# State space layer of a two-layer decoder step: sample states in one run over four row groups, and the silu of B's convolution moved into the next turn

## The chip, the cores and the metric

The kernel runs on one core of a Trainium2 chip. The metric is the device time of one execution in microseconds; lower is better. The median of three runs is 2458.46 us (2457.54 to 2460.95).

## The reference, cut to what matters

One inference step of a two-layer decoder for a prompt of 512 tokens and a sample group of 8 sequences with 8 new tokens each, 576 tokens side by side. Four half SwiGLU networks, a state space (Mamba-2) layer and an attention layer follow one another. The change is in the state space layer alone. Per group of 4 heads, with the prompt cut in chunks of 128 tokens and each sample sequence a chunk of its own:

```python
xc = silu(conv_b + sum(xpad[:, k:k + l] * conv_w[k] for k in range(CONV_W)))   # split into x, B and C
a_cum = cumsum(dt * a)                       # inside the chunk
decay = exp(a_cum[q] - a_cum[s]) where s <= q
wts = (C @ B.T) * decay * dt                 # [q, s] per head
y = wts @ x + (C @ h_prev) * exp(a_cum) + d_skip * x
xw = exp(a_cum[-1] - a_cum) * dt * x
states = B.T @ xw                            # 128 x 64 per head and chunk
h = exp(a_cum[-1]) * h_prev + states         # ssm_prompt, ssm_sample
g = y * silu(z); g = g * rsqrt(mean(g * g)) * norm_g
x += g @ w_out
```

## The kernel before

Every large product is made of float32 operands split in a high and a low part (fp32r): weights arrive raw (`raw`, two slots), ScalarE casts the high part (`high_part`, L939, tile `wh`), GpSimd subtracts it for the low part (`low_part`, L782, tile `wl`), and TensorE multiplies high by high (L1523), high by low (L1524) and low by high (L1531). A unit is a 128 x 1024 block of weights; a slot of `raw` is loaded again by SP's queue when GpSimd is done with it.

The layer runs over 8 groups g. Group 0 is written out, groups 1 to 6 are one hardware loop (called turns 1 to 6 here), group 7 is written out. Each engine has its own program, ordered by hand, and they meet by counting semaphores. In turn g the projections of group g+1 are made ahead (`ahead(0)` to `ahead(5)`: two tiles of x, B, C, and two gate tiles) and the out-projection of group g-1 (`back(0)`, `back(1)`) is made behind.

TensorE's order in a turn: `decays(g)` (L1764, four banks 4 to 7, waits for the square root and for the fourth add of the sample states of the turn before), `back(0)`, `sample_decays` (L1768), `ahead(0)`, `turn` (L1778 transposes x, x and B tile by tile, each waiting for the silu of its tile, `xc_ready`; L1782 transposes the sample tokens), `ahead(1)`, `chunk_sums` (C times B, L1790, and for the samples L1792; chunk states L1798), `back(1)`, `ahead(2)`, `outputs` (L1810, L1820, L1823, for the samples L1828), `ahead(3)`, `states(g, 0)` (L1885), `ahead(4)` with `group_sums` (L1893) in its middle, `states(g, 1)` (L1885), `ahead(5)`.

The sample states: the 64 sample tokens of a group lie on 64 partitions, and `bd` holds B once for each of 4 sequences, masked to the tokens of sequence n and n + 4. A product of 32 partitions with `xws` gives one sequence's state. Two row groups of 32 partitions hold sequences 0 to 3 and 4 to 7. `states(g, half)` makes four sequences, in banks 6 and 7; VectorE adds them to `h0` by two adds (`sample_states`, L2873) before the other half may use the banks.

VectorE's order at the end of a turn: the outputs (`ysb`), `ahead(3)` (projection output to `xp`, L2685 to L2687), the sum of the squares (L2879, input of L1893), `sample_states(0)`, reciprocal (L2902), gain (L2905), `sample_states(1)`, `ahead(4)` (L2707), the low part of the gated output (L2913), `conv(g+1, 2)` (three taps, L2698), `ahead(5)` (L2707), then in the next turn `back(0)` to `back(3)` (L2727).

ScalarE: casts `high_part` (L939); at a turn's end the square root (L1343), silu of the two x tiles, casts of the gated output (L1355), gate silu, silu of B's convolution (`conv_out(g+1, 2)`), gate silu; at a turn's start the cast for `ahead(0)`, `exp_cum` for four heads (L1282, L1284), a cast, exponentials (L1304, L1291, L1308), the cast for `back(1)`, silu of C's convolution (`conv_out(g, 3)`, L1254, L1257, L1258).

SP's queue issues in order: `store_samples` (L639) waits for the four adds of a group, and behind it stand the weights' loads of the next turn's `ahead(0)` and `ahead(1)` (L565).

Before the loop VectorE computes dt and its sums, `state_coefs` (L2665 to L2670) and `head_rows` (L2714, tile `acm`), and GpSimd clears the padding (L822, L823), copies the convolution state (L831) and then makes the low parts.

## Time and profile before

| | |
|---|---|
| median of three runs | 2458.46 us |
| profiled execution, first to last instruction | 2457.2 us |
| TensorE matmul busy | 2421.8 us (99%) |
| VectorE busy | 1856.6 us (76%) |
| ScalarE busy | 1391.8 us (57%) |
| GpSimd busy | 731.7 us (30%) |
| the state space layer | about 392 to 943 us of the span |
| mean granted TensorE clock | 0.994 |

Busy time counts instructions, not waits. TensorE's products overlap in the records: the next one starts before the one before has ended. A row of the timeline gives the start from the span's beginning, the time from the first start to the last end of the merged instructions, engine, line, operation, output and inputs by the program's names, tile shape (rows*columns of the array), operand shape, count, and in brackets the idle time before it and what ended it.

### The profile page before, as it was taken

What the parts mean: (1) busy time and instruction counts of PE and PEld (TensorE: products, weight loads), DVE (VectorE), ACT (ScalarE), POOL (GpSimd) and SP (SyncE); (2) the same over time, 40 slices, a digit from 0 to 9 for tenths busy, and PEclk for the clock granted to TensorE, in tenths of its full rate; (3) what the DMA queues carried; (4) which work ended last, traced back from release to release, by engine and by line L of the source; (5) the groups of instructions that cost most, each with busy time, mean ns of one, the idle gap of its engine ahead of it and who ended that gap; (6) DMA issues with size and microseconds to landing.
All of it is one profiled execution on the core that took longest, in us unless ns stands there. A gap on an engine that the chain in (4) does not pass through costs nothing.

```text
span 2457.2 us, 50185 instructions
## 1 busy us (share of the span) xinstructions
PE 2421.8 (99%) x19713; PEld 2363.8 (96%) x19713; DVE 1856.6 (76%) x3053; ACT 1391.8 (57%) x2388; POOL 731.7 (30%) x672
## 2 busy tenths in 40 slices
PE   8999999999999999999999999999999999999998
PEld 8999999889999989999999999999999997999998
DVE  8979767988888888978876988875235438988875
ACT  7757553645555556757665767664222227767663
POOL 1222233444454532222223222224322321222222
PEclk9999999999999998999999999999999999999999
DMA  6677743123333325677665676763443334677762
GB/s 191 163 169 172 167 119 114 47 95 106 105 101 102 97 88 132 167 160 172 159 146 128 161 168 165 173 150 124 157 141 124 136 110 105 161 170 163 173 149 89
DMA packets 105558, 339.00 MB, mean 138 GB/s; under 512 B 13648, under 2 KB 17232, under 8 KB 87056
## 3 DMA queue, kind: packets, MB, share of 16 engines
q1 hardware_dynamic: 53808, 242.38, 30.0%
q0 software_dynamic: 51552, 93.87, 22.7%
q8 instruction: 137, 2.24, 0.4%
q14 instruction: 61, 0.50, 0.1%
HBM read 223.04 MB, written 19.32 MB: 99 GB/s over the span
## 4 chain that ended last, share of the span: by engine, by line
PE 92%; DVE 4%; DMA 1%; ACT 1%; issue 0%; SPq 0%; DVEq 0%; ACTq 0%
PE ps L1627 17%; PE ps L1625 17%; PE ps L1635 17%; PE ps L1523 7%; PE ps L1531 7%; PE ps L1524 7%; PE ps L1644 2%; PE ps L1645 2%; PE ps L1652 2%; PE ps L1966 1%; PE ps L1967 1%; PE ps L1968 1%; PE ps L1574 1%; DMA sb_lw<-sb_rawf 1%; PE ps L1564 1%; PE ps L1565 1%
## 5 line engine op out<-in xcount | busy, mean ns | idle before, releaser
L1627 PE MATMUL ps<-sb_ual,sb_hw 128*128 128x288 f32 x2240 | 612.8, 295 | 0.0
L1625 PE MATMUL ps<-sb_uah,sb_hw 128*128 128x288 f32 x2240 | 609.5, 295 | 0.2
L799 POOL DMA_DIRECT2D sb_lw<-sb_rawf x328 | 282.2, 866 | 961.6 <-ACT sb_lw L970 944.9
L1625 PEld LDWEIGHTS ps<-sb_uah,sb_hw 128*128 128x128 f32 x2240 | 420.9, 188 | 0.9 <-issue 0.7
L1627 PEld LDWEIGHTS ps<-sb_ual,sb_hw 128*128 128x128 f32 x2240 | 421.2, 188 | 0.0
L1635 PE MATMUL ps<-sb_uah,sb_lw 128*128 128x288 f32 x2240 | 384.8, 293 | 1.1 <-DMA sb_lw<-sb_rawf 1.0
L782 POOL TENSOR_TENSOR sb_wl<-sb_raw,sb_wh 128x1024 fp32r<-128x1024 f32 (+1 forms) x106 | 259.2, 2449 | 412.6 <-ACT sb_wh L939 399.0
L1523 PE MATMUL ps<-sb_uh,sb_wh 128*128 128x288 f32 x1360 | 374.2, 302 | 0.4 <-DVE sb_zs L2707 0.2
L1524 PE MATMUL ps<-sb_ul,sb_wh 128*128 128x288 f32 x1360 | 366.6, 296 | 0.0
L1635 PEld LDWEIGHTS ps<-sb_uah,sb_lw 128*128 128x128 f32 x2240 | 327.9, 188 | 2.3 <-DMA sb_lw<-sb_rawf 1.8
L1523 PEld LDWEIGHTS ps<-sb_uh,sb_wh 128*128 128x128 f32 x1360 | 255.7, 188 | 10.3 <-issue 7.0
L968 ACT CAST sb_hw<-sb_rawf 128x512 fp32r<-128x512 f32 x336 | 207.7, 618 | 86.8 <-PE ps L1635 74.9
L1524 PEld LDWEIGHTS ps<-sb_ul,sb_wh 128*128 128x128 f32 x1360 | 255.8, 188 | 0.5
L1627 PE MATMUL ps<-sb_hl,sb_hw 128*128 128x288 f32 x896 | 244.0, 295 | 0.0
L1625 PE MATMUL ps<-sb_hh,sb_hw 128*128 128x288 f32 x896 | 243.2, 294 | 0.0
L939 ACT CAST sb_wh<-sb_raw 128x1024 fp32r<-128x1024 f32 (+1 forms) x106 | 111.9, 1056 | 176.5 <-PE ps L1531 120.8
L2328 DVE TENSOR_TENSOR sb_lw<-sb_tw,sb_hw 128x1024 fp32r<-128x1024 f32 x112 | 137.1, 1224 | 93.3 <-ACT sb_hw L1005 89.1
L970 ACT ACTIVATE sb_lw<-sb_rawf 128x512 fp32r<-128x512 f32 x328 | 206.4, 629 | 0.0
L1531 PE MATMUL ps<-sb_uh,sb_wl 128*128 128x288 f32 x1360 | 195.4, 296 | 0.0
L1005 ACT CAST sb_hw<-sb_tw 128x1024 fp32r<-128x1024 f32 x112 | 117.8, 1052 | 124.1 <-PE ps L1635 124.1
L1531 PEld LDWEIGHTS ps<-sb_uh,sb_wl 128*128 128x128 f32 x1360 | 186.1, 189 | 0.7 <-issue 0.7
L1627 PEld LDWEIGHTS ps<-sb_hl,sb_hw 128*128 128x128 f32 x896 | 168.4, 188 | 0.0
(357 smaller groups left out, 5118.2 us busy)
## 6 DMA issues: line engine op xcount, KB each, us to landing
sb_lw<-sb_rawf POOLq DMA_DIRECT2D x358, 256.0 KB, 3.7
sb_rawf<-w_ffn_in SPq DMA_DIRECT2D x87, 1024.0 KB, 5.0
sb_rawf<-w_ffn_so SPq DMA_DIRECT2D x32, 1024.0 KB, 5.0
sb_raw<-w_ssd SPq DMA_DIRECT2D x64, 512.0 KB, 3.6
sb_raw<-w_att SPq DMA_DIRECT2D x40, 512.0 KB, 3.7
sb_rawf<-w_ffn_out SPq DMA_DIRECT2D x32, 384.0 KB, 3.1
sb_h<-state SPq DMA_DIRECT2D x8, 1024.0 KB, 4.9
ssm_sample<-sb_h SPq DMA_DIRECT2D x8, 1024.0 KB, 4.8
```

Of the source, the lines that this page charges most:

```text
L782: pool.tensor_tensor(wl[parity][:, 0:width], raw[:, parity, 0:width], wh[parity][:, 0:width].bitcast(F32), ALU.subtract).then_inc(wl_done, 1)
L799: pool.dma_start(slot(lw, p), rawf[:, s % 2, i * BL:(i + 1) * BL], accum_op=ALU.add).then_inc(ld_in[i], 16)
L968: nc.scalar.copy(slot(hw, p), src).then_inc(hd_done, 1)
L970: nc.scalar.activation(slot(lw, p), src, ACT.Copy, scale=-1.0).then_inc(nd_done, 1)
L1005: nc.scalar.copy(slot(hw, 7, 2), tw[:, 2 * BL:4 * BL]).then_inc(ht34_done, 1)
L1523: pe.matmul(ps[:, b, 0:n], w, rh[:, k, t0:t0 + n], start=first and k == 0, stop=False)
L1524: pe.matmul(ps[:, b, 0:n], w, rl[:, k, t0:t0 + n], start=False, stop=False)
L1531: ins = pe.matmul(ps[:, b, 0:n], w, rh[:, k, t0:t0 + n], start=False, stop=last and k == nk - 1)
L1625: pe.matmul(out, w[:, k * P:(k + 1) * P], high[k], start=begins and k == 0, stop=False, skip_group_check=True)
L1627: pe.matmul(out, w[:, k * P:(k + 1) * P], low[k], start=False, stop=False, skip_group_check=True)
L1635: ins = pe.matmul(out, v[:, k * P:(k + 1) * P], high[k], start=False, stop=k == 3, skip_group_check=True)
L2328: V.tensor_tensor(slot(lw, 7, 2), tw[:, 2 * BL:4 * BL], slot(hw, 7, 2).bitcast(F32), ALU.subtract).then_inc(lt34_done, 1)
```

## The change

The sample tokens of x and B are written in spaced rows: sequence b takes rows 16 b to 16 b + 7 of 128, the other rows stay zero. So each 32 rows hold two sequences, `bd` holds B only twice, and all eight states come from one run of eight products over four row groups, into banks 4 to 7. The run stands once, behind `ahead(4)`, and waits for the square root, which reads banks 4 and 5; the last group has two runs of four products. Everything with sample tokens on its partitions (`sgs`, `xds`, `xws`, `cbs`, the masks) has 128 partitions instead of 64. The silu of x and B for the samples writes to `xsp` and `bsp`, cleared once by GpSimd before the layer (with part of `bt`, through which the token-major coefficients are spaced by three copies in `state_coefs`). VectorE adds all four pairs in one place, behind the gain; `ahead(3)` goes behind the sum of squares, and `ahead(5)` ahead of `conv(g+1, 2)`. On ScalarE `conv_out(., 2)` of B goes from the end of a turn to the next turn, behind the exponentials and ahead of C's, and the cast for `back(1)` goes behind both.

```diff
-            bd = at("bd", [SMP, NB // 2, NST])
+            bd = at("bd", [P, 2, NST])
+            xsp = at("xsp", [P, 2, P])
...
-            sgs = at("sgs", [SMP, HPG, SMP])
+            sgs = at("sgs", [P, HPG, SMP])
...
-            xds = at("xds", [SMP, HPG, PD])
-            xws = at("xws", [SMP, HPG, PD])
-            cbs = at("cbs", [SMP, SMP])
+            xds = at("xds", [P, HPG, PD])
+            xws = at("xws", [P, HPG, PD])
+            cbs = at("cbs", [P, SMP])
...
+        def spaced(ap):
+
+            return ap.rearrange("p (b s) -> p b s", s=2 * NS)[:, :, 0:NS]
+
+        def samples_of(i):
+
+            return bsp[:, :] if i == 2 else xsp[:, i, :]
+
         def of_residue(ap, r):
...
             return (0, P) if last and i else (7, 2 * P * i)
 
-        def state_bank(half, rg, last):
-
-            return ((2, 3), (6, 7))[half][rg] if last else 6 + rg
+        def state_bank(rg, last):
...
+                pool.memset(xsp[:, :, :].rearrange("p i r -> p (i r)"), 0.0)
+                pool.memset(bt[0:HEADS, 0:3 * P], 0.0)
+                pool.memset(bsp[:, :], 0.0).then_inc(rows_zero, 1)
 
                 def conv_state(g):
 
...
                         nc.scalar.activation(smp(cz[:, :], 32)[:, :, 0:NS], new, ACT.Silu, bias=bias)
-                    nc.scalar.activation(smp(xc[:, k, SEQ:TOK]), new, ACT.Silu, bias=bias).then_inc(xc_ready, 1)
+                    dst = smp(xc[:, k, SEQ:TOK]) if k == 3 else spaced(samples_of(k))
+                    nc.scalar.activation(dst, new, ACT.Silu, bias=bias).then_inc(xc_ready, 1)
 
                 def gate_out(g, k):
...
                     nc.scalar.activation(s2, s2, ACT.Exp).then_inc(es_done, 1)
+                    conv_out(g, 2)
+                    conv_out(g, 3)
                     if not last and not first:
                         high_part(g, 8, U_LOOP + 3, UW)
-                    if first:
-                        conv_out(g, 2)
-                    conv_out(g, 3)
                     act.wait_ge(t_mm, g * 4 + 3)
                     nc.scalar.copy(bt[:, :], ps[:, 7, :]).then_inc(turned_out, 1)
...
                     if not last:
                         gate_out(g + 1, 0)
-                        conv_out(g + 1, 2)
                         gate_out(g + 1, 1)
                 high_part(0, 8, U_GRP + 1, UW)
...
                 nc.scalar.activation(t2, t2, ACT.Exp).then_inc(coef_exp, 1)
                 high_part(0, 8, U_GRP + 6, UW)
+                act.wait_ge(rows_zero, 1)
                 gate_out(0, 0)
                 conv_out(0, 0)
...
                         for i in range(3):
-                            ins = pe.transpose(ps[0:SMP, 4, rows(i)], xc[:, i, SEQ:TOK], ident[:, :])
+                            ins = pe.transpose(ps[:, 4, rows(i)], samples_of(i), ident[:, :])
                         ins.then_inc(t_mm, 1)
...
                     pe.wait_ge(xs_done, g + 1)
-                    pe.matmul(ps[0:SMP, 4, 0:SMP], xc[:, 2, SEQ:TOK], xc[:, 3, SEQ:TOK],
+                    pe.matmul(ps[:, 4, 0:SMP], samples_of(2), xc[:, 3, SEQ:TOK],
                               start=True, stop=True).then_inc(cb_mm, 1)
 
...
                         ins.then_inc(y_mm, 1)
 
-                def states(g, half, last=False):
+                def states(g, last=False, row_groups=(0, 1, 2, 3)):
 
                     if last:
-                        pe.wait_ge(so_evac, g * 8 + 1)
-                        if half:
-                            pe.wait_ge(y_evac, g * 2 + 2)
-                    elif half == 0:
+                        pe.wait_ge(*((y_evac, g * 2 + 2) if 2 in row_groups else (so_evac, g * 8 + 1)))
+                    else:
                         pe.wait_ge(y_evac, g * 2 + 2)
-                    else:
-                        pe.wait_ge(ss_evac, g * 4 + 2)
+                        pe.wait_ge(gsqrt_ready, g + 1)
                     for k in range(2):
-                        for rg in range(2):
+                        for rg in row_groups:
                             r = slice(32 * rg, 32 * rg + 32)
-                            ins = pe.matmul(ps[:, state_bank(half, rg, last), k * 256:k * 256 + 256], bd[r, 2 * half + k, :],
+                            ins = pe.matmul(ps[:, state_bank(rg, last), k * 256:k * 256 + 256], bd[r, k, :],
                                             xws[r, :, :].rearrange("p j d -> p (j d)"), start=True, stop=True)
                     ins.then_inc(ss_mm, 1)
...
-                        n = P if c < CH else SMP
+                        tokens = src[:, rows(c)] if c < CH else bt[0:HEADS, rows(q)]
                         col = (q * (CH + 1) + c) * HEADS
-                        ins = pe.transpose(ps[0:n, 4, col:col + HEADS], src[:, c * P:c * P + n], ident[0:HEADS, 0:HEADS])
+                        ins = pe.transpose(ps[:, 4, col:col + HEADS], tokens, ident[0:HEADS, 0:HEADS])
                 ins.then_inc(dtok_mm, 1)
                 def group(g, first):
...
-                    states(g, 0)
                     ahead(4, lambda: group_sums(g))
-                    states(g, 1)
+                    states(g)
                     ahead(5)
 
...
-                states(g, 0, True)
+                states(g, True, (0, 1))
                 token_sums(g, 0)
-                states(g, 1, True)
+                states(g, True, (2, 3))
                 token_sums(g, 1)
                 keep_busy(3)
...
-                    V.memset(tok[:, :, :, :].rearrange("p q c h -> p (q c h)"), 0.0)
                     V.tensor_copy(onr[:, :], ones[0:H2, :])
                     dve.wait_ge(dt_exp, 1)
...
                     dve.wait_ge(coef_exp, 1)
-                    V.tensor_tensor(t2, t2, t0, ALU.mult).then_inc(dtok_in, 1)
+                    step(V.tensor_tensor(t2, t2, t0, ALU.mult))
+                    dve.wait_ge(rows_zero, 1)
+                    for q, src in enumerate((acT, t0, t2)):
+                        ins = V.tensor_copy(spaced(bt[0:HEADS, rows(q)]), smp(src[0:HEADS, SEQ:TOK]))
+                    ins.then_inc(dtok_in, 1)
 
                     hi = acm[:, 0, :]
...
                     v = ps[:, 4, 0:3 * (CH + 1) * HEADS].rearrange("p (q c h) -> p q c h", q=3, c=CH + 1)
-                    V.tensor_copy(tok[:, :, 0:CH, :], v[:, :, 0:CH, :])
-                    V.tensor_copy(tok[0:SMP, :, CH, :], v[0:SMP, :, CH, :])
+                    V.tensor_copy(tok[:, :, :, :], v)
                     step(V.tensor_copy(acT[:, :], acm[:, 0, :].bitcast(F32)))
 
...
-                                        gtok[0:SMP, q, CH, :].unsqueeze(2).broadcast_to([SMP, HPG, PD]), ALU.mult)
-                    half = [SMP, NB // 2, NST]
-                    V.tensor_tensor(bd[:, :, :], ps[0:SMP, 4, 2 * P:3 * P].unsqueeze(1).broadcast_to(half),
-                                    maskb[:, :].unsqueeze(2).broadcast_to(half), ALU.mult).then_inc(xs_done, 1)
+                        V.tensor_tensor(dst[:, :, :], ps[:, 4, 0:2 * P].rearrange("p (j d) -> p j d", j=HPG),
+                                        gtok[:, q, CH, :].unsqueeze(2).broadcast_to([P, HPG, PD]), ALU.mult)
+                    both = [P, 2, NST]
+                    V.tensor_tensor(bd[:, :, :], ps[:, 4, 2 * P:3 * P].unsqueeze(1).broadcast_to(both),
+                                    maskb[:, :].unsqueeze(2).broadcast_to(both), ALU.mult).then_inc(xs_done, 1)
                     def states():
                         dve.wait_ge(st_mm, g * 2 + 1)
                         dve.wait_ge(st_h, g * 16 + 16)
...
-                        ins = V.scalar_tensor_tensor(ysb[:, i, SEQ:TOK], xc[:, i, SEQ:TOK], dk,
-                                                     sample_out(i), ALU.mult, ALU.add)
+                        ins = V.scalar_tensor_tensor(smp(ysb[:, i, SEQ:TOK]), spaced(samples_of(i)), dk,
+                                                     smp(sample_out(i)), ALU.mult, ALU.add)
                         ins.then_inc(y_evac, 1)
                         dve.wait_ge(y_evac, g * 2 + (i + 1))
...
                         V.tensor_tensor(ysb[:, i, :], ysb[:, i, :], zs[:, i, :], ALU.mult).then_inc(gz_ready, 1)
-                    if not last:
+                    if first:
                         ahead(3)
 
-                    def sample_states(half, row_groups=(0, 1)):
-                        dve.wait_ge(ss_mm, g * 2 + half + 1)
+                    def sample_states(row_groups):
+                        dve.wait_ge(ss_mm, g + (2 if 2 in row_groups and last else 1))
                         for rg in row_groups:
-                            b = 4 * rg + 2 * half
+                            b = 2 * rg
                             dve.wait_ge(hm_done, g * 8 + b + 2)
-                            V.tensor_tensor(h0[:, b:b + 2, :], h0[:, b:b + 2, :], two(ps[:, state_bank(half, rg, last), :]),
+                            V.tensor_tensor(h0[:, b:b + 2, :], h0[:, b:b + 2, :], two(ps[:, state_bank(rg, last), :]),
                                             ALU.add).then_inc(ss_evac, 1)
 
 
                     if not last:
                         dve.wait_ge(gsq_done, g * 2 + 2)
                         V.tensor_tensor(zs[:, 0, :], zs[:, 0, :], zs[:, 1, :], ALU.add).then_inc(gsum_done, 1)
-                        sample_states(0)
                         if first:
                             conv(1, 1)
...
+                            ahead(3)
                     if last:
                         v = acc[0:TW, 0, 0:TB]
                         dve.wait_ge(gn_mm, g + 1)
...
                     if not last:
-                        sample_states(1)
+                        sample_states(range(4))
                         ahead(4)
                     for i in range(2):
...
-                        ahead(5)
                     else:
-                        sample_states(0, (1,))
+                        sample_states((1,))
                         for m in range(KD):
                             back(g, m)
                             if m:
                                 side(1, m - 1)
                             else:
-                                sample_states(1)
+                                sample_states((2, 3))
                         side(1, KD - 1)
...
         "ones": np.ones((P, P), f), "ident": np.eye(P, dtype=f), "mask": np.triu(np.ones((P, P), f)),
-        "mask_smp": (np.triu(np.ones((SMP, SMP))) * (s[:, None] // NS == s[None, :] // NS)).astype(f),
-        "mask_block": (s[:, None] // NS % (NB // 2) == np.arange(NB // 2)[None, :]).astype(f),
+        "mask_smp": ((a[:, None] // 16 == s[None, :] // NS) * (a[:, None] % 16 <= s[None, :] % NS)).astype(f),
+        "mask_block": (a[:, None] // 16 % 2 == np.arange(2)[None, :]).astype(f),
         "keep": np.tile(keep, (H2, 1)), "one_head": np.tile(np.eye(HEADS, dtype=f), (2, 1)), "dist": np.concatenate(tables, 1).astype(f),
         "dist_smp": np.concatenate(cols, 1).astype(f), "slopes": np.tile(slopes, (P, 1)), "slopes_smp": sls.astype(f),
```

## Rows read from the trace of the kernel before

Turn 2 runs from 566.36 to 632.78 us, turn 3 from there to 699.27.

**Rows 1.** Busy time of each engine by stretch, granted clock, DMA share (us, instructions).
```profile
504.00:508.00 4.00, 4.00 (x23) 3.70 (x23) 1.11 (x2) 3.99 (x13) 1.58 (x1) 0.77 0.53 181
562.00:629.00 67.00, 67.00 (x533) 63.37 (x532) 54.60 (x100) 34.72 (x61) 32.46 (x29) 1.00 0.30 97
```

**Rows 2.** Waits of TensorE, whole run: total, times, longest (us).
```profile
PE ps L1764 <- DVE sb_acm L2714: 3.6, 1, 3.6
...
PE ps L1966 <- DVE sb_zs L2707: 2.0, 1, 2.0
```

**Rows 3.** Timeline of TensorE, turns 2 and 3: start, us, instruction [idle before].
```profile
604.90 1.07 PE L1810 MATMUL ps<-sb_h,sb_cz 128*32 128x256 f32 x16
...
608.79 0.44 PE L1823 MATMUL ps<-sb_er,sb_hst 128*64 128x128 f32 x4
609.15 0.45 PE L1828 MATMUL ps<-sb_sgs,sb_xds 64*64 64x64 f32 x8
...
616.52 1.13 PE L1885 MATMUL ps<-sb_xws,sb_bd 32*128 32x256 f32 x8
...
619.83 1.13 PE L1893 MATMUL ps<-sb_zs,sb_ones 128*128 128x288 f32 x4
...
632.78 1.20 PE L1764 MATMUL ps<-sb_acm,sb_onr 64*128 64x512 f32 x4
...
647.25 1.47 PE L1778 MATMUL ps<-sb_ident,sb_xc 128*128 128x128 f32 x12
```

**Rows 4.** Timeline of VectorE, end of turn 2.
```profile
617.43 1.51 DVE L2879 TENSOR_TENSOR sb_zs<-sb_zs 128x576 f32<-128x576 f32 x1
...
621.77 3.75 DVE L2902 RECIPROCAL sb_gnr<-sb_gnr 128x576 f32<-128x576 f32 x1 [1.63 <-ACT sb_gnr L1343]
...
627.12 1.28 DVE L2873 TENSOR_TENSOR sb_h<-sb_h,ps 128x512 f32<-128x512 f32 x2
```

**Rows 5.** Timeline of GpSimd in the same stretch.
```profile
615.44 5.75 POOL L782 TENSOR_TENSOR sb_wl<-sb_raw,sb_wh 128x1024 fp32r<-128x1024 f32 x2
```

**Rows 6.** Timeline of ScalarE, turn 3.
```profile
636.00 1.03 ACT L939 CAST sb_wh<-sb_raw 128x1024 fp32r<-128x1024 f32 x1
...
647.87 1.10 ACT L939 CAST sb_wh<-sb_raw 128x1024 fp32r<-128x1024 f32 x1
...
650.28 0.72 ACT L1254 ACTIVATE sb_xc<-sb_acc,sb_cw 128x512 f32<-128x512 f32 x1
650.91 0.33 ACT L1257 ACTIVATE sb_cz<-sb_acc,sb_cw 128x64 f32<-128x64 f32 x1
```

**Rows 7.** Timeline of SP's queue, end of turn 2; landing of the weights' load (L565).
```profile
628.56 0.36 SPq L639 DMA_DIRECT2D ssm_sample<-sb_h  x1
629.19 1.73 SPq L565 DMA_DIRECT2D sb_raw<-w_ssd  x2
...
DMA to landing us min/median/max: 5.4/5.4/5.4
```

**Rows 8.** Timelines before the loop: GpSimd, TensorE, VectorE.
```profile
396.94 0.31 POOL L823 MEMSET sb_cz<- 128x256 f32 x1
...
397.79 4.76 POOL L782 TENSOR_TENSOR sb_wl<-sb_raw,sb_wh 128x1024 fp32r<-128x1024 f32 x2
...
400.33 0.83 PE L1531 MATMUL ps<-sb_uh,sb_wl 128*128 128x288 f32 x5
...
432.13 2.84 DVE L2670 TENSOR_TENSOR sb_acm<-sb_acT,sb_acm 32x576 fp32r<-32x576 f32 x1
```

**Rows 9.** Timelines around the start of turn 1: VectorE, TensorE, ScalarE.
```profile
494.54 1.27 DVE L2873 TENSOR_TENSOR sb_h<-sb_h,ps 128x512 f32<-128x512 f32 x2
...
495.96 1.17 PE L1764 MATMUL ps<-sb_acm,sb_onr 64*128 64x512 f32 x4 [1.08 <-DVE sb_h L2873]
...
502.07 1.05 ACT L939 CAST sb_wh<-sb_raw 128x1024 fp32r<-128x1024 f32 x1 [0.18 <-DMA sb_raw<-w_ssd]
...
514.34 1.47 PE L1778 MATMUL ps<-sb_ident,sb_xc 128*128 128x128 f32 x12
```

More of the change, by code:

```diff
@@ L266, in step_kernel @@
             mask = at("mask", [P, P])
-            masks = at("masks", [SMP, SMP])
-            maskb = at("maskb", [SMP, NB // 2])
+            masks = at("masks", [P, SMP])
+            maskb = at("maskb", [P, 2])
+            at("pad_mb", [P, 2])
             cz = at("cz", [P, NB * 32])
-            at("pad_h0", [P, 320])
+            bsp = at("bsp", [P, P])
+            at("pad_h0", [P, 320 - P])
             h0 = at("h0", [P, NB, HPG * PD])
@@ L351, in step_kernel @@
         conv_done, xc_ready, zs_ready = sem("conv_done"), sem("xc_ready"), sem("zs_ready")
-        tap_done = sem("tap_done")
+        tap_done, rows_zero = sem("tap_done"), sem("rows_zero")
         acm_ready, rs_mm, r_mm = sem("acm_ready"), sem("rs_mm"), sem("r_mm")
@@ L546, in old_bank @@
             return (0, P) if last and i else (7, 2 * P * i)
-        def state_bank(half, rg, last):
-            return ((2, 3), (6, 7))[half][rg] if last else 6 + rg
+        def state_bank(rg, last):
+            return (2, 3, 6, 7)[rg] if last else 4 + rg
         def head_bank(t, last):
@@ L1918, in last_chunk_sums @@
                     pe.wait_ge(xs_done, g + 1)
-                    pe.matmul(ps[0:SMP, 4, 0:SMP], xc[:, 2, SEQ:TOK], xc[:, 3, SEQ:TOK],
+                    pe.matmul(ps[:, 4, 0:SMP], samples_of(2), xc[:, 3, SEQ:TOK],
                               start=True, stop=True).then_inc(cb_mm, 1)
@@ L2744, in group @@
                     for j in range(HPG):
-                        ins = V.tensor_scalar(sgs[:, j, :], ps[0:SMP, 4, j * SMP:(j + 1) * SMP], gtok[0:SMP, 0, CH, j:j + 1],
+                        ins = V.tensor_scalar(sgs[:, j, :], ps[:, 4, j * SMP:(j + 1) * SMP], gtok[:, 0, CH, j:j + 1],
                                               0.0, ALU.subtract, ALU.min)
@@ L2806, in group @@
                     dve.wait_ge(cb_mm, g + 1)
-                    V.tensor_tensor(cbs[:, :], ps[0:SMP, 4, 0:SMP], masks[:, :], ALU.mult)
+                    V.tensor_tensor(cbs[:, :], ps[:, 4, 0:SMP], masks[:, :], ALU.mult)
                     V.tensor_tensor(cbm[:, :].rearrange("p (c q) -> p c q", c=CH), ps[:, 5, :].rearrange("p (c q) -> p c q", c=CH),
@@ L2883, in group @@
                             head_rows(1)
+                        else:
+                            ahead(3)
                     if last:
@@ L2894, in group @@
                                         v.unsqueeze(2).broadcast_to(each), ALU.mult).then_inc(gsum_done, 1)
-                        sample_states(0, (0,))
+                        sample_states((0,))
                         dve.wait_ge(gn_mm, g + 2)
@@ L2914, in group @@
                     if not last:
+                        ahead(5)
                         conv(g + 1, 2)
-                        ahead(5)
                     else:
-                        sample_states(0, (1,))
+                        sample_states((1,))
                         for m in range(KD):
```

3 lines of the change are left out of this document (1 added, 2 removed).

## Prediction

> **What bounds the kernel now.** I read the busy time by stretch first, then TensorE's waits, then one turn of the state space loop engine by engine. In the stretch of one turn [rows 1] TensorE is busy for all of 67.00 us at a granted clock of 1.00, VectorE for 54.60, ScalarE for 34.72, GpSimd for 32.46. So inside the loop every microsecond that TensorE works less is a gain, but only if nothing else comes late instead. The list of TensorE's waits [rows 2] has hardly anything of this layer in the loop; what it has lies before it: 3.6 us until the head rows (`acm`) of group 0 are made, and 2.0 us in turn 1 until a gate projection is evacuated. Turn 3 begins at 632.78 with L1764 [rows 3]; call that instant T.
>
> **TensorE's part.** Today each half of the sample states costs 1.13 us, eight overlapping records from 616.52 on and as many after `ahead(4)` [rows 3]. Afterwards there is one run of sixteen records over four row groups. That four strips run side by side is not shown for row groups; for four column strips it is: L1810's sixteen records of the same 256 columns take 1.07 us [rows 3]. I take 1.13 us for the new run, so one half goes: -1.13 us in each of the groups 0 to 6 (the last group keeps two runs). Bounds: if only two row groups overlap, the run takes 2 x 1.13 and nothing is gained.
> Beside it, products of 64 rows become products of 128 rows. L1828 is the one whose tile shape then agrees with its neighbours'; four records of L1823 start at 608.79, and L1828 only at 609.15 [rows 3]. Those four take 0.44 us overlapped, so by their spacing the next would fit near 609.0, and I estimate that about 0.15 us a turn is a change of shape that goes away. With L1792, whose shape also widens, I take -0.2 us a turn, bounds 0 and -0.3. The transposes L1782 keep their number.
> The Trainium skill, TensorEngine Tiling (Array Packing), section Tiling Modes, says that row tiles load and multiply in parallel and that a change of tiling mode drains the engine; the rows above agree as far as they go. Its section PSUM Bottleneck says that tiling speeds up TensorE and not the evacuation, which speaks against this change, and here it is the adds below that it is about.
>
> **The sum of squares comes 0.3 us late.** `states(g, 0)` goes from before `ahead(4)`, so the group sums L1893 in its middle would start at 619.83 - 1.13 = 618.70. They need L2879, which runs from 617.43 for 1.51 us [rows 4], while GpSimd's two subtractions run back to back from 615.44, 2.87 us each [rows 5], the first until 618.3. The operation behind L2879 has its usual 0.6 us only after that. The change takes `ahead(3)` from before L2879, so that it may be issued 0.5 us earlier, but it would still end at 618.94. So TensorE waits 0.3 us, and what hangs on the sums (square root, L2902) comes 1.13 - 0.3 = 0.83 us earlier, not 1.13. Bounds: 0 to 0.4 us.
> The Trainium skill, SBUF — State Buffer, section SBUF: two separate sides, states that VectorE with two SBUF inputs and GpSimd hold their common port one after the other for a whole instruction; by that rule L2879 can't end before 618.8, and L2879's 1.51 us agrees. If they shared it evenly, the 0.3 us would be zero.
>
> **VectorE's adds and the SP queue.** Today the second pair of adds L2873 starts at 627.12 and takes 1.28 us [rows 4], 5.35 us after the reciprocal's start at 621.77. Afterwards all four stand there: from 621.77 - 0.83 + 5.35 = 626.29 for 2.5 us, until 628.8, against 628.4 today. Removing two adds earlier in the turn wins nothing at this place, because VectorE waits there for the square root. The first queue behind them is SP's: `store_samples` waits for the fourth add, and the next group's first projection weights are queued behind it. It is issued at 628.56, the weights' load 0.63 us behind, and they land 5.4 us after that [rows 7], at 634.6, T + 1.8. Afterwards: store at 628.95, landing at 635.0. T itself moves to 632.78 - 0.83 = 631.95. So the weights land at T + 3.0, where ScalarE casts them today at 636.00 = T + 3.2 [rows 6].
> Thus putting B's silu and its wait out of ScalarE's way at the head of the turn (the gate's silu then has only L2707 before it) lets ScalarE begin the turn's chain only 0.2 us earlier: the next late thing is the DMA. VectorE's `ahead(5)` before `conv(g+1,2)` also moves `back(0)` behind three convolution taps; the third out-projection product may wait up to 0.7 us for it. That is inside the next wait, not added to it.
>
> **B's silu behind the exponentials.** `turn(g)` transposes three tiles; the third, B, waits for B's silu. The first tile starts at 647.25 [rows 3], eight transposes at 0.11 us later B's turn is at 648.12 = T + 15.34. ScalarE today has cast at 636.00, ended the exponentials at 647.87 (when the next cast starts), cast for 1.10 and started the silu of C at 650.28, so a table load of 1.3 us lies between [rows 6]. Afterwards the cast goes behind the silus, so the silu of B starts 1.3 us after the exponentials and lasts 0.72 + 0.33 with an overlap, 0.96: it ends at 647.87 + 1.30 + 0.96 = 650.13, which is 14.13 us after the first cast. With that cast at T + 3.0 it is T + 17.15. TensorE then waits 17.15 - 15.34 = 1.8 us for what was ready long before. Bounds: 0.6 us if the cast could follow the gate's silu at T + 1.8; 2.0 us if it stays where it is today. I take 1.8, the row nearest to it being the landing. C's silu comes no later than today (it loses a cast of 1.10 ahead of it and gains 0.96), the cast for `back(1)` comes some 2.3 us later but is needed only after `ahead(1)`, and `outputs` (L1810) starts only 28 us before a turn's end [rows 3], some 20 us behind C's silu, so that GpSimd's four decay products have room.
> A full turn thus changes by -0.83 - 0.2 + 1.8 = +0.77 us.
>
> **Before the loop.** GpSimd gets three more memsets ahead of `conv_state(0)` and of its first subtraction at 397.79 [rows 8]. The one of 256 columns takes 0.31 us; three of 256, 384 and 128 columns make 0.9 one by one, and I take 0.75 as they overlap a little. The first subtraction (half of 4.76) ends at 400.2 and L1531 starts at 400.33, so 0.7 us goes through to the first convolution input, and from there along VectorE to `acm`, for which TensorE waits anyway 3.6 us [rows 2]. `state_coefs` gets three copies (0.4 to 0.5 us) ahead of the two operations of which the second, L2670, takes 2.84 us because it starts at 432.13 beside a GpSimd subtraction [rows 8]; both will then stand behind that. +0.5. The memset of `tok` goes where VectorE waits for ScalarE next: nothing. Together +1.2, bounds 0.3 and 1.8.
>
> **From group 0 into turn 1.** There the two adds start at 494.54 and TensorE waits until 495.96 for them [rows 9]. With four of them turn 1 starts 1.1 us later, since what precedes them on VectorE (a convolution and the head rows) is in line with the same GpSimd subtractions and doesn't start earlier for good: +1.1, bounds -1.2 and +1.2. In turn 1 the cast is at 502.07, 6.1 us after the start [rows 9], also for a landing; B's silu ends 14.13 later, 20.2 after the start. Its transposes stand today at 514.34 + 0.87 = 515.21, 19.25 after the start. So +1.0, -0.2 for the shapes. The 2.0 us wait for the gate goes, but it lies before this wait and is swallowed.
>
> **The last group.** Turn 6 still ends 0.83 us earlier after its own start of the sample states. In the last group B's silu stands before C's; of its 0.96 us VectorE's own queue hides a part, I take +0.45 (0 to 0.96). Together -0.4.
>
> **Sum.** +1.2 before the loop, +1.1 +1.0 -0.2 for group 0 and turn 1, 5 x 0.77 = +3.8 for turns 2 to 6, -0.4 at the end: +6.5 us. The profiled span of 2457.2 us becomes 2463.7. The median of the runs is 2458.46, 1.3 above that span (one execution, and what lies around it), so 2465.0 us.
>
> **Rivals.** (1) As forecast, 0.50: 2460.5 to 2469.5, by the bounds above.
> (2) Half as late, 0.20: the weights land earlier or the chain of exponentials is quicker, so that the wait for B is near its low bound 0.6. A turn is then -0.83 - 0.2 + 0.6 = -0.4, six turns -2.4, and with +1.2 and +1.1 the kernel is where it was: 2456 to 2461.
> (3) The other side, 0.12: TensorE alone decides. The place is the silu of B against T + 15.34; it decides from a first cast before T + 1.2, which needs a landing 1.8 us earlier than I work out. Then turns 1 to 6 give 6 x (-1.03), the 2.0 us wait in turn 1 goes, and +2.3 stays: -5.9, 2452.6 (2450 to 2454). For it: ScalarE is idle before B's silu today and could start sooner. Against it: the landing is bound to the fourth add.
> (4) The clock, 0.13: after the waits around turn 1 the granted clock was 0.77 in the stretch 504 to 508 [rows 1], that is, part of it at the level of 1.2 GHz, although 2.0 us was the longest single wait. If waits of 1.8 us in every turn, or the one of some 3 us in turn 1, bring this on repeatedly, each fall costs about half of 3.5 us. Two to six of them: 2469 to 2476.
> (5) The change doesn't do what it says, 0.05: four row groups don't overlap. TensorE loses another 0.85 us in the run of sixteen, but it stands before the wait for B, which shrinks with it: 2464 to 2468.
> About 0.2%, 4.9 us, is what a measurement tells from no change. Of (1) some 0.36 lies above 2463.4 and 0.14 within; (4) and most of (5) are slower, (2) is within, (3) is faster: faster 0.12, same 0.35, slower 0.53. The range 2456 to 2472 leaves out (3) and the top of (4).
>
> **What would show it.** In the profile after: L1885 with sixteen records in 1.1 to 1.3 us once a turn (TensorE's part); a wait of L1893 for `zs` of 0.3 us; four adds in a row ending 0.4 us later after L1764's turn start than now; the first cast of each turn waiting for the DMA at T + 3.0; and above all L1778 waiting 1 to 1.8 us in each loop turn for ScalarE's B tile. A loop turn should be 0.7 to 0.8 us longer than now. If L1778 doesn't wait, the forecast is wrong and (3) or (2) holds. If the turn start waits for `h` in the loop, the adds are longer than I took them.

## The result and the profile after

The changed kernel takes 2470.51 us (median of 4 runs, 2468.54 to 2470.93), the kernel before 2458.76 (4 runs). The ratio is 1.0044, with a 95% interval of 1.003 to 1.0059: slower by 11.75 us, where +6.5 was forecast. The profiled execution has a span of 2468.9 us against 2457.2, so the traces carry the whole difference.

The busy time by stretch tells how much lies in the loop. The columns are the stretch, its length, then the busy time of TensorE, its weight loads, VectorE, ScalarE and GpSimd, the granted clock, and the DMA share. First the changed kernel: around the start of turn 0, around the start of turn 1, turn 3, and turns 2 to 6 together.

```profile
444.00:452.00 8.00, 6.66 (x22) 5.42 (x23) 6.45 (x9) 7.49 (x22) 2.35 (x1) 0.57 0.23 66
499.00:507.00 8.00, 7.11 (x28) 6.30 (x29) 6.61 (x10) 2.36 (x3) 0.00 (x0) 0.57 0.80 288
638.19:705.91 67.72, 65.59 (x527) 62.19 (x526) 53.11 (x99) 34.37 (x60) 31.98 (x28) 1.00 0.29 96
...
570.59:908.72 338.13, 327.68 (x2631) 310.78 (x2630) 266.94 (x492) 171.87 (x300) 159.87 (x140) 1.00 0.29 96
```

The same of the kernel before:

```profile
444.00:452.00 8.00, 8.00 (x42) 6.92 (x43) 7.65 (x13) 7.74 (x24) 2.68 (x2) 0.79 0.22 66
...
566.36:898.59 332.23, 332.23 (x2632) 314.11 (x2631) 270.97 (x491) 171.15 (x300) 159.97 (x140) 1.00 0.31 98
```

Before, TensorE never stood still in turns 2 to 6. After, it has 4.55 us less to do in them (332.23 - 327.68) and stands still for 10.45 (338.13 - 327.68): 5.9 us longer, 1.18 a turn. The granted clock is 1.00 in both stretches, so the clock has no part in this. Its waits name what for (total, times, longest):

```profile
PE ps L1792 <- ACT sb_bsp L1273: 10.0, 7, 2.3
...
PE ps L1778 <- DVE sb_h L2885: 3.3, 1, 3.3
PE ps L1977 <- DVE sb_x L2739: 2.2, 6, 0.5
...
PE ps L1904 <- DVE sb_zs L2891: 1.8, 7, 0.3
```

One turn's worth of TensorE's timeline, from the end of turn 2 (the answer to [rows 3]; L1896 was L1885, L1904 was L1893, L1778 was L1764, L1792 was L1778):

```profile
625.08 1.24 PE L1904 MATMUL ps<-sb_zs,sb_ones 128*128 128x288 f32 x4 [0.25 <-DVE sb_zs L2891]
...
630.52 1.15 PE L1896 MATMUL ps<-sb_xws,sb_bd 32*128 32x256 f32 x16
...
638.19 1.20 PE L1778 MATMUL ps<-sb_acm,sb_onr 64*128 64x512 f32 x4
...
642.46 0.29 PE L1979 MATMUL ps<-sb_gh,sb_wl 128*128 128x288 f32 x1
643.00 0.40 PE L1977 MATMUL ps<-sb_gh,sb_wh 128*128 128x288 f32 x1 [0.25 <-DVE sb_x L2739]
643.24 0.29 PE L1978 MATMUL ps<-sb_gl,sb_wh 128*128 128x288 f32 x1
643.38 0.30 PE L1979 MATMUL ps<-sb_gh,sb_wl 128*128 128x288 f32 x1
...
653.22 1.04 PE L1792 MATMUL ps<-sb_ident,sb_xc 128*128 128x128 f32 x8
655.87 0.65 PE L1792 MATMUL ps<-sb_ident,sb_xc 128*128 128x128 f32 x4 [1.61 <-ACT sb_bsp L1273]
```

The sixteen records of L1896 take 1.15 us where eight took 1.13. The stop for B's tile is there, 1.61 us. A stop also costs more than its length: starts of neighbouring products are 0.13 us apart, so the three steps from 642.46 to 643.38 would take 0.4 us and took 0.92, 0.52 lost for a shown wait of 0.25. The rest, some 0.3 us, is overlap: the product before the stop runs out alone, and the one behind it is followed only 0.24 us later. That is called refilling below; the runs tell what it costs, not what causes it.

ScalarE in turn 3 (the answer to [rows 6]) and VectorE around its start (the answer to [rows 4]):

```profile
641.32 1.06 ACT L953 CAST sb_wh<-sb_raw 128x1024 fp32r<-128x1024 f32 x1 [1.04 <-DMA sb_raw<-w_ssd]
...
652.90 0.57 ACT L1323 ACTIVATE sb_sgs<-sb_sgs 128x256 f32<-128x256 f32 x1
653.49 1.28 ACT L1268 ACT_TABLE_LOAD   x1
654.78 0.72 ACT L1268 ACTIVATE sb_xc<-sb_acc,sb_cw 128x512 f32<-128x512 f32 x1
655.41 0.33 ACT L1273 ACTIVATE sb_bsp<-sb_acc,sb_cw 128x64 f32<-128x64 f32 x1
```

```profile
622.90 2.12 DVE L2891 TENSOR_TENSOR sb_zs<-sb_zs 128x576 f32<-128x576 f32 x1 [0.75 <-ACT sb_zs L1349]
...
632.47 2.48 DVE L2885 TENSOR_TENSOR sb_h<-sb_h,ps 128x512 f32<-128x512 f32 x4
634.86 0.76 DVE L2719 TENSOR_TENSOR sb_zs<-ps,sb_rms 128x576 f32<-128x576 f32 x1
635.78 3.10 DVE L2926 TENSOR_TENSOR sb_gl<-sb_ysb,sb_gh 128x576 fp32r<-128x576 f32 x2 [0.17 <-ACT sb_gh L1369]
638.81 0.74 DVE L2719 TENSOR_TENSOR sb_zs<-ps,sb_rms 128x576 f32<-128x576 f32 x1
```

The first cast waits for its weights until T + 3.1 (T = 638.19), and B's transposes begin 14.55 us after it (655.87 - 641.32). Behind the adds, `gl` takes 3.10 us for its two halves, from 635.78 on; it ends at T + 0.7.

The starts of turns 0, 1 and 7 in the changed kernel, and of turns 0 and 7 in the one before:

```profile
445.34 2.07 PE L1778 MATMUL ps<-sb_acm,sb_onr 64*128 64x512 f32 x4 [3.49 <-DVE sb_acm L2726]
...
499.89 2.04 PE L1778 MATMUL ps<-sb_acm,sb_onr 64*128 64x512 f32 x4 [3.31 <-DVE sb_h L2885]
...
908.72 0.49 PE L1778 MATMUL ps<-sb_acm,sb_onr 64*128 64x512 f32 x1
```

```profile
443.92 0.82 PE L1764 MATMUL ps<-sb_acm,sb_onr 64*128 64x512 f32 x2 [3.55 <-DVE sb_acm L2714]
...
898.59 0.73 PE L1764 MATMUL ps<-sb_acm,sb_onr 64*128 64x512 f32 x2
```

Of the 11.7 us, 1.4 are there at the start of turn 0, 2.5 come in group 0, 0.3 in turn 1, 5.9 in turns 2 to 6, and 1.6 behind turn 7's start.

### The profile page after: what moved, and what is told of

Its sections match the earlier page's. It is cut to its first block, busy times and chain, and to the rows that moved or that the text cites. A ratio compares the mean times of both kernels' runs of the same rounds, so it can differ in the third digit from the quotient of the medians.

```text
span 2468.9 us, 50196 instructions
## 1 busy us (share of the span) xinstructions
PE 2417.6 (98%) x19713; PEld 2361.5 (96%) x19713; DVE 1853.2 (75%) x3054; ACT 1392.7 (56%) x2388; POOL 732.8 (30%) x675
## 4 chain that ended last, share of the span: by engine, by line
PE 79%; DVE 9%; ACT 5%; DMA 3%; issue 3%; DVEq 0%; SPq 0%; ACTq 0%; POOL 0%
PE ps L1641 16%; PE ps L1639 16%; PE ps L1649 16%; PE ps L1545 5%; PE ps L1537 4%; PE ps L1538 4%; PE ps L1658 2%; PE ps L1659 2%; PE ps L1666 2%; DMA sb_raw<-w_ssd 2%; ACT sb_sg L1299 1%; PE ps L1588 1%; DVE sb_acc L2710 1%; PE ps L1578 1%; PE ps L1579 1%
## 5 line engine op out<-in xcount | busy, mean ns | idle before, releaser
L1639 PEld LDWEIGHTS ps<-sb_hh,sb_hw 128*128 128x128 f32 x896 | 168.1, 188 | 0.7 <-issue 0.7
```

The source lines that it names most:

```text
L1639: pe.matmul(out, w[:, k * P:(k + 1) * P], high[k], start=begins and k == 0, stop=False, skip_group_check=True)
```

## Experiments

Two theories stood first. **A**: the loop's loss is B's silu behind the exponentials, whose chain begins at a cast bound to the load behind the four adds. **B**: the four adds in a row cost by themselves. The first four kernels were to tell them apart. For each kernel the table gives the ratio to the kernel before and, from its trace, turns 2 to 6: their length and TensorE's busy time, both over 5.

| kernel | median us | ratio (95%) | turn us | busy us |
|---|---|---|---|---|
| before | 2458.76 | 1 | 66.45 | 66.45 |
| changed | 2470.51 | 1.0044 (1.003 to 1.0059) | 67.63 | 65.54 |
| e1 | 2463.39 | 1.0013 (1.0004 to 1.0021) | 66.96 | 65.37 |
| e2 | 2467.66 | 1.0034 (1.002 to 1.0047) | 67.52 | 66.68 |
| e3 | 2472.52 | 1.0051 (1.0038 to 1.0065) | 68.35 | 65.64 |
| e4 | 2468.48 | 1.0029 (1.0018 to 1.004) | 67.39 | 65.63 |
| e5 | 2461.25 | 1.0000 (0.9991 to 1.0009) | 65.97 | 65.36 |
| e6 | 2457.22 | 0.9991 (0.9981 to 1.0001) | 65.63 | 65.18 |
| e7 | 2455.85 | 0.9978 (0.9969 to 0.9987) | 65.66 | 65.22 |
| e8 | 2458.21 | 0.9990 (0.9982 to 0.9999) | 66.45 | 66.45 |
| e9 | 2471.69 | 1.0050 (1.0037 to 1.0063) | 68.24 | 65.91 |

Beside e1 to e9 the kernel before ran at 2460.4 to 2460.5 on its chips, so the ratios are to be compared, not the medians.

**e1: the single run alone.** B's silu is back at the turn's end, `conv(g + 1, 2)` stands ahead of `ahead(5)` again, and the third cast ahead of C's silu; `ahead(3)` stays behind the sum of squares.

```diff
                         gate_out(g + 1, 0)
+                        conv_out(g + 1, 2)
                         gate_out(g + 1, 1)
...
+                        conv(g + 1, 2)
                         ahead(5)
-                        conv(g + 1, 2)
```

> The changed kernel with the sampled states and their sums as changed (one run, four adds in a row), but with silu of B's convolution put back at the turn's end, ahead of the sample tile's, and the casts and convolutions in their former order. Theory A (the loop's loss is B's silu behind the exponentials, and the exponentials begin at a cast that waits for the weights whose transfer is issued behind the four adds): the third pair of transposes no longer waits for sb_bsp, a turn of the loop costs the former 66.45 us less the 1.1 to 1.3 that the one run and the smaller tile save, and at most 1.0 of that is lost to the sum of gate 5 standing behind the convolution; 2453 to 2459 us. Rival B (the four adds in a row and the later transfers cost by themselves): it stays at 2467 to 2471 us.

It missed: 66.96 us a turn, where its sum allows 65.15 to 66.35 (66.45 less 1.1 to 1.3, plus at most 1.0). The wait for B is gone, as A has it, but TensorE now stops 1.40 us for the gate's sum of `ahead(5)`:

```profile
637.22 0.40 PE L1979 MATMUL ps<-sb_gh,sb_wh 128*128 128x288 f32 x1 [1.40 <-DVE sb_zs L2721]
```

```profile
633.68 0.83 DVE L2712 SCALAR_TENSOR_TENSOR sb_acc<-sb_xp,sb_cw,sb_acc 128x600 f32<-128x600 f32 x1
634.67 1.83 DVE L2712 SCALAR_TENSOR_TENSOR sb_acc<-sb_xp,sb_cw,sb_acc 128x600 f32<-128x600 f32 x2 [0.15 <-DVE sb_acc L2712]
636.42 0.75 DVE L2721 TENSOR_TENSOR sb_zs<-ps,sb_rms 128x576 f32<-128x576 f32 x1
```

In the kernel before `gl` began at T - 3.8; here (T = 632.85) VectorE leaves it only at 633.68, T + 0.8. TensorE has 1.13 us less to do before T, and VectorE has two more adds in front of `gl`, and both push the same way. This stop is the one that e1's text had at 1.0 us at most. The single run alone costs 0.5 us a turn.

**e2: B's silu alone, with the former two runs of states.** The same lines the other way round, in the kernel before.

> The kernel before, with its two rounds of states, and only silu of B's convolution moved behind the next turn's exponentials. Theory A: B's tile reaches the transposes 17.1 to 17.6 us behind the start of the turn instead of being there, the first transposes of B wait 1.5 to 2.3 us, a turn costs 0.9 to 2.3 us more than before and the kernel 2464 to 2472 us. Rival B (the one run and its adds in a row are what costs): 2458 to 2460 us. Rival C (the order alone costs, whatever time the weights land): 2464 to 2472 us as well, and e3 then brings nothing.

It costs 1.07 us a turn and gives 1.0034, within A's forecast for the time, though the wait is shorter than forecast (0.77 to 0.90 us in turns 2 to 6, not 1.5 to 2.3):

```profile
639.18 1.06 ACT L939 CAST sb_wh<-sb_raw 128x1024 fp32r<-128x1024 f32 x1 [0.37 <-DMA sb_raw<-w_ssd]
```

```profile
653.66 0.65 PE L1776 MATMUL ps<-sb_ident,sb_xc 128*128 128x128 f32 x4 [0.90 <-ACT sb_xc L1258]
```

From the cast to B's transposes it is 14.48 us, as in the changed kernel; the cast comes at T + 1.95 (T = 637.23), where it waits 0.37 us for its load. So each part is slower than before when alone: B as the sole cause falls with e2, and A as the sole cause with e1.

**e3: the load ahead of the samples' store on SyncE's queue.**

```diff
-                    store_samples(g - 1)
                     part(1, io["w_ssd"][g + 1, 0])
+                    store_samples(g - 1)
```

> The changed kernel, with the load of the next turn's first weights issued on SyncE's queue ahead of the store of the sampled outputs instead of behind it. Theory A: the first cast is no longer bound to a landing at T+3.0 us but follows its own engine at about T+2.1, the wait for sb_bsp falls from 1.6 to about 0.6 us, a turn takes about 66.7 us instead of 67.6 and the kernel about 2465 us (2463 to 2467). Rival C (the order of ScalarE's work costs, not the landing): no change, 2470 us.

Here my own theory failed in time while its mechanism held. The cast comes at T + 2.1 (turn 3, T = 636.22) without a wait for its load, and no wait for `sb_bsp` is left, but the turn is longer, 68.04 us in turn 4:

```profile
638.31 1.04 ACT L953 CAST sb_wh<-sb_raw 128x1024 fp32r<-128x1024 f32 x1
```

```profile
712.55 0.40 PE L1977 MATMUL ps<-sb_gh,sb_wh 128*128 128x288 f32 x1 [2.41 <-DVE sb_x L2739]
```

```profile
707.98 3.85 DVE L2710 SCALAR_TENSOR_TENSOR sb_acc<-sb_xp,sb_cw,sb_acc 128x600 f32<-128x600 f32 x2 [0.15 <-DVE sb_acc L2710]
```

```profile
708.82 2.38 POOL L793 TENSOR_TENSOR sb_wl<-sb_raw,sb_wh 128x1024 fp32r<-128x1024 f32 x1 [3.69 <-ACT sb_wh L953]
```

(ScalarE in turn 3; TensorE, VectorE and GpSimd in turn 4.) The cast releases GpSimd's low part, and it now falls onto VectorE's convolution taps: two of them take 3.85 us where they take 1.83 otherwise, 2.02 more, and `back` behind them is late for TensorE. The Trainium skill, SBUF — State Buffer, section SBUF: two separate sides, has VectorE (with both inputs from SBUF) and GpSimd hold their common port one after the other, a whole instruction long; this row agrees, since the loss is the low part's 2.38 us less a small rest.

**e4: B's silu between the first cast and the exponentials.**

```diff
                         proj(0)
+                    if not first:
+                        conv_out(g, 2)
                     for j in range(HPG):
                         exp_cum(j)
...
-                    conv_out(g, 2)
+                    if first:
+                        conv_out(g, 2)
```

> The changed kernel, with silu of B's convolution between the turn's first cast and the exponentials (one queue place earlier by 11 us of ScalarE's work, the same tables and the same states in one run). Theory A: sb_bsp is written at about T+5.3, the exponentials begin about 1.4 us later and still end ahead of what waits for them, no wait at the transposes of B is left, a turn takes 65.5 to 65.9 us and the kernel 2457 to 2461 us. Rival B (adds in a row and later transfers): 2468 to 2470 us. A second way to miss: an added table load and the later exponentials delay the states' decay products, which would show as a wait of TensorE further on in the turn, and 2462 to 2468 us.

A's number failed again (67.39 us a turn, not 65.5 to 65.9); the second way to miss came true: no wait for B, but a stop of 1.07 us 31 us into the turn.

```profile
669.45 0.40 PE L1980 MATMUL ps<-sb_gh,sb_wh 128*128 128x288 f32 x1 [1.07 <-DVE sb_x L2742]
```

```profile
665.92 2.82 DVE L2829 TENSOR_TENSOR sb_sg<-sb_sg,sb_cbm 128x512 f32<-128x512 f32 x1
668.66 0.74 DVE L2742 TENSOR_TENSOR sb_x<-sb_x,ps 128x576 f32<-128x576 f32 x1
669.32 0.68 DVE L2829 TENSOR_TENSOR sb_sg<-sb_sg,sb_cbm 128x512 f32<-128x512 f32 x1
```

```profile
659.79 6.03 POOL L884 TENSOR_TENSOR sb_er<-sb_er,sb_xc 128x512 f32<-128x512 f32 x4
665.79 2.39 POOL L793 TENSOR_TENSOR sb_wl<-sb_raw,sb_wh 128x1024 fp32r<-128x1024 f32 x1
```

It is the same collision at another place: L2829 takes 2.82 us instead of 0.68 beside a low part that starts at 665.79. From here on a theory **D** took the place of A and B: TensorE's own work in a turn is some 65 us; each stop adds its length and the refilling; and what makes the stops is when the casts release GpSimd's low parts, and which VectorE instruction they meet.

**e5: e4, and the third cast back ahead of C's silu.**

```diff
+                    if not last and not first:
+                        high_part(g, 8, U_LOOP + 3, UW)
                     if first:
                         conv_out(g, 2)
                     conv_out(g, 3)
-                    if not last and not first:
-                        high_part(g, 8, U_LOOP + 3, UW)
```

> The kernel with silu of B's convolution ahead of the exponentials, and ScalarE's cast of the turn's third weight tile put back ahead of silu of C's convolution, as it was before the change. Theory D (found in the runs so far: a turn is 65.0 us of TensorE's own work plus each stop and about 0.3 us of refilling behind it; the stop 31 us into the turn, 1.07 us for sb_x of line 2742, comes from GpSimd's low part and products that run later because that cast runs later, and hold up VectorE's products): that stop goes, a turn takes 66.0 to 66.2 us instead of 67.4, and the kernel 2458.5 to 2461 us. Rival: the stop comes from VectorE's own order and stays; 2467 to 2470 us.

As D has it: 65.97 us a turn (66.11 in turn 3), the stop at 31 us is gone, ratio 1.0000. One ScalarE cast moved from behind C's silu to ahead of it is worth 1.4 us a turn (67.39 - 65.97).

**e6: e5, and the first load of a turn ahead of the convolution state's store.** (`store_conv(g)` goes behind `part(0)` of the next turn; the last group likewise.)

```diff
                     part(0, io["w_ssd"][g - 1, 6])
+                    store_conv(g)
                     store_prompt(g - 1)
...
-                    store_conv(g + 1)
```

> As e5, and SyncE issues the load of the weight tile of the next turn's start ahead of the store of the convolution's new state, instead of behind it. Theory D: the cast that stands ahead of the casts of sb_gh on ScalarE no longer waits 2.5 us but about 1 us for its landing, sb_gh is there when VectorE asks for it, GpSimd's low part no longer runs under VectorE's subtractions (2.7 instead of 3.1 us for the two), and the stop of 0.40 us 5 us into the turn goes, with its 0.3 us of refilling: a turn of 65.3 to 65.6 us, the kernel 2454 to 2457.5 us. Rival: VectorE's four adds in a row set that stop whatever the landing is; no change against e5.

65.63 us a turn and 0.9991 (0.9981 to 1.0001), not clearly faster than before. ScalarE's cast and VectorE's `gl`:

```profile
625.85 1.04 ACT L953 CAST sb_wh<-sb_raw 128x1024 fp32r<-128x1024 f32 x1
```

```profile
626.82 2.47 DVE L2888 TENSOR_TENSOR sb_h<-sb_h,ps 128x512 f32<-128x512 f32 x4
629.22 0.75 DVE L2722 TENSOR_TENSOR sb_zs<-ps,sb_rms 128x576 f32<-128x576 f32 x1
629.88 1.41 DVE L2929 TENSOR_TENSOR sb_gl<-sb_ysb,sb_gh 128x576 fp32r<-128x576 f32 x2
```

The cast doesn't wait, the low part runs under the adds, which read PSUM and are not held up, and `gl` takes 1.41 us instead of 3.10, more than the 0.4 I had expected of it. In the loop the four adds in a row, still there, stop nothing any more: the only waits of 0.25 us or more left in turns 2 to 6 are the sums' of 0.26 to 0.28. At the end of group 0 TensorE still waits 1.12 us for them, against 1.08 before.

**e7: e6, and in group 0 the adds ahead of the gains.**

```diff
+                    if first:
+                        sample_states(range(4))
                     for i in range(2):
...
-                        sample_states(range(4))
+                        if not first:
+                            sample_states(range(4))
```

> As e6, and in the first group alone VectorE adds the sampled states between the reciprocal and the gains instead of behind the gains. TensorE's wait of 3.1 us for these adds at the end of the first group becomes one of some 2 us for sb_gl, 1.2 us further on: 0.5 to 2.5 us less than e6. A miss would be none at all: then the end of the first group is set by sb_gl in either order.

1.4 us less in the medians (2455.85 against 2457.22), which their spreads don't separate well; in the trace TensorE waits 1.32 us for `gl` and 1.08 for `back`, and the clock stays at 1.00 from 498 to 513, where e6 had 0.77. Against the kernel before it is faster by 0.22% (0.13 to 0.31%).

**e8: the load's order of e6 alone, in the kernel before.**

> The kernel before with the same edit alone. It tells how much of what e6 and e7 gain belongs to the sampled states' single run and how much to the order of the load. Theory D: a turn of the old kernel has no stop of TensorE to fill, so it stays at 66.45 us; only group 0 gains, where the gains take 3.3 us beside GpSimd's low part instead of 1.5: turn 1 starts 1.5 to 1.9 us earlier, but TensorE has only 1.1 us of waiting there to give back; 2456.5 to 2459 us. Rival: the load's order is all of the gain of e6 and e7; 2452 to 2456 us.

Turns stay at 66.45 us, as expected, and only what lies around group 0 gains: 0.999 (0.9982 to 0.9999). So by the medians about half of e7's 0.22% is the load's order and the other half what the single run gives once its collisions are gone, but the two intervals overlap (e7's ends at 0.9987), so the halves are not measured apart. What the traces do show is the loop: 65.66 us a turn in e7 against 66.45 here, 4.0 us in turns 2 to 6, of which some 1.2 go back before the loop.

**e9: the same edit alone, in the changed kernel.**

> The changed kernel with one edit of e6 alone: SyncE issues the load of the weight tile of the next turn's start ahead of the store of the convolution's new state. Theory D: sb_gh is early, GpSimd's low part no longer stretches VectorE's subtractions, so the stop for sb_x of line 2739 goes from each turn (0.25 us and its refilling, together 0.5), but the wait for sb_bsp stays at 1.6 to 1.9 us, because the first cast of a turn is still bound to the load behind the store of the samples: a turn of 67.1 to 67.3 us, the end of group 0 some 2 us earlier (the gains no longer run beside GpSimd), and the kernel 2464.5 to 2468 us. Rival: with the head of the turn quicker the wait for sb_bsp takes up all of it; 67.6 us a turn, 2467.5 to 2470.5 us.

The rival was right about the turn; its time was 1.2 us short (2471.69 against 2470.5 at most, on chips where the kernel before takes 1.7 us more than in the first runs). The stop for `sb_x` is gone in turns 2 to 6, and the wait for B takes all of it:

```profile
587.17 0.97 PE L1792 MATMUL ps<-sb_ident,sb_xc 128*128 128x128 f32 x4 [1.99 <-ACT sb_bsp L1273]
...
656.35 0.65 PE L1792 MATMUL ps<-sb_ident,sb_xc 128*128 128x128 f32 x4 [2.08 <-ACT sb_bsp L1273]
```

Turn 3 takes 67.63 us (67.72 in the changed kernel). The changed kernel's period is a ring: first cast at T + 3.1, B's tile 14.55 us on, and the next T 50.0 us behind that (705.91 - 655.87); e9 has the same three figures (3.1, 14.55 and 50.0). What TensorE saves inside the ring it waits off at B's tile. And these longer stops were followed by the lower level of the clock in two of the five turns, as rival (4) had it; those turns took 69.10 and 69.17 us, and that is why the mean is 68.24:

```profile
586.00:592.00 6.00, 4.83 (x26) 4.84 (x27) 4.82 (x11) 4.24 (x9) 2.85 (x2) 0.72 0.29 87
569.59:638.69 69.10, 66.83 (x528) 63.64 (x527) 52.82 (x98) 34.36 (x60) 31.54 (x28) 0.98 0.28 93
638.69:706.32 67.63, 65.30 (x527) 62.16 (x526) 51.87 (x98) 34.37 (x60) 31.97 (x28) 1.00 0.29 96
```

## Why the prediction was right, and where it was short

The side was right, and so was the main mechanism; the size was 6.5 for a measured 11.75 us. With 2470.51 us the kernel lies inside the stated range of 2456 to 2472, but 1.0 us above the range of rival (1), the one that names this mechanism, and inside that of (4), whose repeated falls of the clock did not come. So the number held only because the whole range was kept wide enough for (4).

- **TensorE's part** (-1.13 and -0.2 a turn): right. In e6, with hardly a stop, it is busy for 65.18 us a turn against 66.45, -1.27.
- **The sums 0.3 us late**: right (0.25 us); the refilling behind it, about as much again, wasn't in the sum.
- **B's tile, +1.8 us a turn at T + 17.15**: in turn 3 it came at T + 17.68 and the wait was 1.61; over turns 2 to 6 it was 1.31 to 1.61. The chain was 0.4 us longer, 14.55 from cast to transposes instead of 14.13. From the cast to the table load it is 12.17 us (641.32 to 653.49) where 11.87 were taken, since the load starts only when the exponential of 0.57 us before it has ended, and TensorE starts 0.13 us behind the silu's end at 655.74. TensorE itself was later by the next point.
- **"Inside the next wait, not added to it"**: this sentence on `back(0)` failed as a picture, though not by much in the sum. The stop for `sb_x` (0.25 us, 0.5 with refilling) does lie in front of the wait for B and is swallowed by it, as e9 shows. What e1, e3 and e4 show is that it is the next bound as soon as B's wait is gone. I had worked out that VectorE's adds end 0.4 us later; I had not worked out that T comes earlier at the same time, and I left out that `gl`, behind them, takes 3.10 us beside a low part.
- **A turn**: +0.77 forecast, +1.18 measured; five turns 5.9 instead of 3.8. By the ring, the missing 0.4 is the 0.4 of the chain from cast to B's tile: the term of the sum that was too small in the loop. Counted on TensorE it is the same 0.4: it stands still for 2.09 us a turn, as forecast (1.8 + 0.3), but its busy time falls by 0.91 and not by 1.33. In e6, without the stops for `sb_x` and B, it falls by 1.27, so 0.36 a turn goes with these two stops.
- **Before the loop**, +1.2 forecast: turn 0 starts 1.4 us later. A single trace doesn't settle it: the eight kernels with the new part start turn 0 between 444.2 and 446.1 us, 445.3 in the mean, the three with the old one (before, e2, e8) between 443.8 and 444.5, 444.1 in the mean. That is +1.2.
- **Group 0**, +1.1 forecast, +2.5 measured: the term that was sized worst. The adds cost what I took: e1's group 0, with the same code up to these adds, takes 53.27 us against 52.04 before, +1.2. The other 1.3 goes with the clock behind the wait for `acm`, granted at 0.57 over 444 to 452 against 0.79 before and in e1; the sum had no term for it. e3, e4 and e5, which also have more of this stretch at 1.2 GHz than e1, take 54.00, 53.97 and 54.17 us. The wait is as long as it was (3.49 and 3.55 us), and e8, without the single run, is granted 0.67 there; whether the change makes the longer stay at 1.2 GHz more likely stays open. What I had overlooked is that here too the gains of group 0 run beside a low part, before the change (3.34 us for two) as after (3.68): in e6 they take 1.55, and its group 0 is 1.7 us shorter than e5's.
- **Turn 1**: the +0.8 of the sum leaves out the 0.83 us by which turn 2 starts earlier, and these stand in the -0.4 of the end. From start to start turn 1 was forecast at 0.0 and measured at +0.3; the wait for B there is 2.29 us.
- **The end**: counted in the same way +0.4 was forecast behind turn 7's start, and it is +1.6. No run here takes this apart; the stretch behind turn 7's start is 1557 to 1564 us long in all these traces, so 1.6 us lies within what it varies by.
- **The rivals**: (3), TensorE alone, is what e6 and e7 come near in the loop (65.2 us busy in a turn of 65.6), at 2456 to 2457 us beside 2460.4 for the kernel before, and only after three other queues had been put in order. (5) is refuted by L1896's 1.15 us. (4) did not come in the loop, where the granted clock is 1.00 throughout; around the start of turn 1 it is 0.57 over 499 to 507 against 0.79 before.

## What to carry to other kernels

In a loop whose period is a ring through several queues, a saving on the busiest engine can be worth nothing until the ring is found: write down who releases whom from one turn's start to the next, and ask how long each link is. An engine that shares a port (GpSimd here, 2.4 us at a time) is placed by whoever releases it, so moving a cast or a load by one place moves a collision; look which VectorE instruction it will meet, and let it meet one that reads PSUM. A stop costs TensorE some overlap of its products as well, here 0.2 to 0.3 us.

## What the runs showed of the hardware

- Sixteen products of 256 columns over four row groups take 1.15 us, as long as eight over two (1.13).
- A VectorE instruction with two SBUF inputs beside a GpSimd subtraction of 2.4 us ends up to 2.1 us late (L2829 at 2.82 instead of 0.68 us, two taps at 3.85 instead of 1.83); additions from PSUM were not touched (e6: 2.47 us for four beside it, as for the four at the end of group 0, which no low part meets).
- Stops of about 2 us, one in each turn, were followed by the 1.2 GHz level in some turns (e9: 0.72 over 586 to 592, the turn 69.10 us) and not in others (67.63 us with a stop of 2.08). e3's stops of 2.4 to 2.5 us were in one turn of five (69.36 us against 68.0 to 68.2), the changed kernel's of 1.3 to 1.6 us in none.
